# A filter stage unrolled in half tiles, and two thirds of a modulation product moved to VectorE in a late stage

## The reference, cut to what matters

```
mod_lat = jnp.split((jax.nn.silu(c) @ w_mod[l] + b_mod[l])[:, None, :], 6, axis=-1)
mod_ctx = jnp.split(jax.nn.silu(c_ctx) @ w_mod[l] + b_mod[l], 6, axis=-1)
u_ctx = modulate(h_ctx, mod_ctx[0], mod_ctx[1])
mix_lat, _ = token_mixer(modulate(h_lat, mod_lat[0], mod_lat[1]), ctx_states, lp, rows)
h_lat = layer_norm(DN_ALPHA * h_lat + mod_lat[2] * mix_lat, ln_g[l, 0], ln_b[l, 0])
ffn_lat = moe_ffn(modulate(h_lat, mod_lat[3], mod_lat[4]), lp)
h_lat = layer_norm(DN_ALPHA * h_lat + mod_lat[5] * ffn_lat, ln_g[l, 1], ln_b[l, 1])

def hyena_filters(n, lp):
    hid = jnp.sin(lp["hy_freq"][0] * (feat @ lp["hy_w1"] + lp["hy_b1"]))     # feat (n, 33), hid (n, 64)
    hid = jnp.sin(lp["hy_freq"][1] * (hid @ lp["hy_w2"] + lp["hy_b2"]))
    filt = (hid @ lp["hy_w3"]) * jnp.exp(-t01 * deltas)                      # (n, 2048)
    filt = filt.reshape(n, HY_ORDER, 2, HY_D)
    fwd, bwd = filt[:, :, 0], filt[:, :, 1]
    k2 = jnp.concatenate([fwd, jnp.zeros((1, HY_ORDER, HY_D), F32), jnp.flip(bwd[1:], axis=0)], axis=0)
    return k2 / jnp.sum(jnp.abs(k2), axis=0, keepdims=True)
```

## Time and profile before

| what | value |
|---|---|
| median of the runs | 3189.16 us (3187.28 to 3192.15) |
| span of the profiled execution, first to last instruction | 3182.9 us |
| TensorE busy in the span | 2769.4 us, 87% |
| VectorE busy | 1631.1 us, 51% |
| ScalarE busy | 996.2 us, 31% |
| GpSimd busy | 279.9 us, 9% |
| mean granted TensorE clock | 0.928 |
| first matmul of `stage_filter_spectrum` (L578) starts at | 188.09 us |
| stretch of the `md` merge | about 2010 to 2152 us |

### The profile page before, as it was taken

The page is one execution under the profiler, slowest core; times in us unless marked ns, Lnnn a source line. Parts: engine busy times, 40 slices in busy tenths (PEclk is TensorE's granted clock), DMA queues, the critical chain, the costliest instruction groups (busy, mean ns, idle before and its releaser), DMA issues. The chain is left out here.

```text
span 3182.9 us, 33378 instructions
## 1 busy us (share of the span) xinstructions
PE 2769.4 (87%) x12400; PEld 2050.8 (64%) x12400; DVE 1631.1 (51%) x1517; ACT 996.2 (31%) x1104; POOL 279.9 (9%) x236
## 2 busy tenths in 40 slices
PE   7889898989999599999894999998918999999973
PEld 4443773335888577878773778784417888888861
DVE  4634336272332256343178262424627888888866
ACT  2302230001332133320000010001007888888860
POOL 1200000000000221000141300000010000000001
PEclk9889999999999788999996999998958999999996
DMA  6432454221232421211110111113149999999945
GB/s 213 132 126 112 166 205 135 89 86 60 67 108 84 135 78 52 71 53 51 40 51 14 47 34 47 43 30 121 50 189 366 371 375 374 371 371 371 373 183 224
DMA packets 92001, 482.89 MB, mean 152 GB/s; under 512 B 10836, under 2 KB 20324, under 8 KB 76745
## 3 DMA queue, kind: packets, MB, share of 16 engines
q1 hardware_dynamic: 71688, 382.41, 33.5%
q0 software_dynamic: 20224, 99.25, 8.3%
HBM read 424.01 MB, written 82.78 MB: 159 GB/s over the span
## 5 line engine op out<-in xcount | busy, mean ns | idle before, releaser
L337 PE MATMUL ps<-uT_upper_rest,ring_rest 128*128 128x512 f32 x1360 | 541.3, 398 | 0.0
L337 PEld LDWEIGHTS ps<-uT_upper_rest,ring_rest 128*128 128x128 f32 x1360 | 259.0, 190 | 66.1
L337 PE MATMUL ps<-uT_upper_rest,cs_upper 128*128 128x512 f32 x320 | 130.2, 407 | 55.0 <-DVE cs_val L1971 46.8
L2443 PE MATMUL ps<-ring_rest,uT_rest 128*128 128x256 f32 (+1 forms) x416 | 135.2, 325 | 26.2 <-DVE uT_upper_rest L2520 26.2
L2445 PE MATMUL ps<-ex_u_raw_rest,uT_rest 128*128 128x256 f32 x560 | 156.6, 280 | 0.0
L2443 PE MATMUL ps<-ex_upper,uT_rest 128*128 128x256 f32 (+1 forms) x424 | 136.3, 322 | 21.0 <-DVE uT_upper_rest L2520 21.0
L337 PE MATMUL ps<-uT_upper_rest,xbc_upper 128*128 128x512 f32 x336 | 136.0, 405 | 6.1 <-DVE ring_rest L727 6.1
L1744 PE MATMUL ps<-sb_merged,ring 128*128 x256 | 114.5, 610 | 26.0 <-DVE sb_merged L1819 26.0
L2444 PE MATMUL ps<-ex_upper,uT_rest 128*128 128x256 f32 (+1 forms) x424 | 134.3, 317 | 0.0
L337 PE MATMUL ps<-uT_rest,xbc_upper 128*128 128x512 f32 x336 | 134.2, 399 | 0.0
L2444 PE MATMUL ps<-ring_rest,uT_rest 128*128 128x256 f32 (+1 forms) x416 | 133.3, 320 | 0.0
(11 more groups left out here) (437 smaller groups left out, 6305.6 us busy)
## 6 DMA issues: line engine op xcount, KB each, us to landing
sb_spare<-in_ex_g SPq DMA_DIRECT2D x35, 2048.0 KB
ex_u_raw<-in_ex_u SPq DMA_DIRECT2D x35, 2048.0 KB
sb_merged<-in_ex_d SPq DMA_DIRECT2D x35, 2048.0 KB, 10.3
ring<-in_w_mod SPq DMA_DIRECT2D x48, 512.0 KB, 4.5
sb_uT<-moe SPq DMA_DIRECT2D x35, 512.0 KB, 12.0
moe<-sb_uT POOLq DMA_DIRECT2D x35, 512.0 KB, 8.0
ring<-in_w_gate SPq DMA_DIRECT2D x32, 512.0 KB, 3.6
ring<-in_dft SPq DMA_DIRECT2D x24, 512.0 KB, 3.6
```

The source lines that it names most:

```text
L337: last = self.nc.tensor.matmul(out, weight, x[:, k, lo:hi], start=(k == 0 and n == 0), stop=(k == kt - 1 and n == 2))
L2443: nc.tensor.matmul(out, left_up, w_up, start=first, stop=False)
```

## The change: what it does, and the diff

The filter stage loses its hardware loop. It is written out in 16 turns, each half a tile: 128 tokens for one of the two filter orders, so 1024 of the 2048 columns. The hidden layers hold tokens 0 to 511 on partitions 0 to 63 and tokens 512 to 1023 on partitions 64 to 127, so the chain of VectorE has 512 columns on 128 partitions; `w2` and `w3` are stored twice, once for each half. The copy to `hid_t` is gone: TensorE takes its weights from `hid` directly. `window`, `filt` and `mags` have two buffers, PSUM three pairs of banks. The scaling of the first tap is done in tile 0 alone. The exponentials for tiles 0 and 1 go ahead of the turns, each later one two tiles ahead. The loads have semaphores of their own: the first layer waits for four small ones.

Only 16 of the 48 modulation items (vectors 0 and 1) are computed there. Their weights are the ring's first segment. Vectors 2 to 5 are accumulated in the `md` merge: GpSimd's queue loads 32 pieces of 128x1024 (512 KB), VectorE multiplies each with a column of `ccs` and adds it to a tile `late` (four rows of 1024 on each partition, with the bias on partition 0). `late` takes the place of `y_aT`, which now lives on through the tail, where the output stage sums its partitions with a matrix of ones and writes the four rows back over it.

```
 @@ stage_filter_time, sync
-                for dst, src in loads:
-                    sp.dma_start(dst, src).then_inc(loaded, 16)
+                for dst, src in ((featT[:, :], a["featT"]), (w1[:, :], a["hy_w1"]), (k.cols[:, :], a["cols"]),
+                                 (w2[:, :], a["hy_w2"])):
+                    sp.dma_start(dst, src).then_inc(feat_in, 16)
+                sp.dma_start(w3[:, :], a["hy_w3"]).then_inc(w3_in, 16)
+                sp.dma_start(k.consts[:, :], a["consts"]).then_inc(consts_in, 16)
+                sp.dma_start(deltas[:, :], a["neg_deltas"][0].partition_broadcast(P)).then_inc(deltas_in, 16)
                 ring.stream(sp)
 @@ tensor
+                def modulation(m):
+                    slot = m % RING
+                    ring.arrived(pe, base, m // RING, slot)
+                    if m >= 4 and m % 2 == 0:
+                        pe.wait_ge(mod_read, m // 2 - 1)
+                    for kt in range(KT):
+                        mm = nc.tensor.matmul(ps[0:2, 6 + m // 2 % 2, (m % 2) * P:(m % 2 + 1) * P], k.ccs[:, kt, :],
...
+                def filters(n):
+                    t, o = halves[n]
+                    h, at = t // 4, t % 4 * P
+                    part = slice(h * HY_HID, (h + 1) * HY_HID)
+                    if n >= 3:
+                        pe.wait_ge(filt_read, n - 2)
+                    for d in range(2):
+                        q = 2 * o + d
+                        mm = nc.tensor.matmul(ps[:, 2 * (n % 3) + d, :], hid[part, 1, at:at + P],
+                                              w3[part, q * HY_D:(q + 1) * HY_D], start=True, stop=True)
+                    mm.then_inc(filt_mm, 1)
...
+                pe.wait_ge(hid_ready, 2)
+                pe.wait_ge(w3_in, 16)
+                for n in range(len(halves)):
+                    filters(n)
+                    if n + 4 < EARLY:
+                        modulation(n + 4)
 @@ scalar
+                decay(0)
+                decay(1)
+                modulated(0)
+                modulated(1)
+                for n in range(len(halves)):
+                    act.wait_ge(filt_ready, n + 1)
+                    if n >= 2:
+                        act.wait_ge(summed, n)
+                    nc.scalar.activation(mags[:, n % 2, :, :], filt[:, n % 2, :, :], ACT.Abs).then_inc(mags_ready, 1)
+                    if n % 2 and n // 2 + 2 < TT:
+                        decay(n // 2 + 2)
+                    if n % 2 and n // 2 + 2 < EARLY // 2:
+                        modulated(n // 2 + 2)
 @@ vector
+                for n, (t, o) in enumerate(halves):
+                    mine = filt[:, n % 2, :, :]
+                    v.wait_ge(filt_mm, n + 1)
+                    v.wait_ge(window_ready, t + 1)
+                    if n >= 2:
+                        v.wait_ge(mags_ready, n - 1)
+                        v.wait_ge(folded, 2 * (n - 1))
+                    nc.vector.tensor_tensor(mine, ps[:, 2 * (n % 3):2 * (n % 3) + 2, :],
+                                            window[:, t % 2, 2 * o * HY_D:2 * (o + 1) * HY_D].rearrange(
+                                                "p (d c) -> p d c", d=2), ALU.mult).then_inc(filt_read, 1)
...
                     for dst, op in ((even, ALU.add), (odd, ALU.subtract)):
+                        nc.vector.tensor_tensor(dst[:, t, o, :], mine[:, 0, :], mine[:, 1, :], op).then_inc(folded, 1)
 @@ stage_merge
+                if late is not None:
+                    pool.wait_ge(late_zero, 1)
+                    lo, hi = ROW_AT["b_late"]
+                    pool.dma_start(late[0:1, :, :].rearrange("p q n -> p (q n)"), a["rows"][:, lo:hi]).then_inc(late_b, 16)
+                    for i in range(KT):
+                        for q in range(LATE):
+                            if i:
+                                pool.wait_ge(late_done, LATE * (i - 1) + q + 1)
+                            pool.dma_start(piece[:, q, :], a["w_late"][i * LATE + q]).then_inc(late_in[q], 16)
...
+                def late_modulation(i):
+                    for q in range(LATE):
+                        v.wait_ge(late_in[q], 16 * (i + 1))
...
+                        nc.vector.scalar_tensor_tensor(out=late[:, q, :], in0=piece[:, q, :], scalar=k.ccs[:, i, 0:1],
+                                                       in1=late[:, q, :], op0=ALU.mult, op1=ALU.add).then_inc(late_done, 1)
                 split_items(0)
+                if late is not None:
+                    nc.vector.memset(late[:, :, :], 0.0).then_inc(late_zero, 1)
...
                         split_items(i + 1)
+                    if late is not None:
+                        late_modulation(i)
                     merge(i)
 @@ stage_output
-                for part in range(4):
-                    for kt in range(KT):
-                        m = (2 + part) * KT + kt
-                        mm = nc.tensor.matmul(ps[:, 2 * part + kt // 4, (kt % 4) * P:(kt % 4 + 1) * P],
-                                              k.mod[:, m, 0:1].broadcast_to([P, P]), k.const("ident"),
+                for part in range(LATE):
+                    for h, (lo, hi) in enumerate(HALVES):
+                        mm = nc.tensor.matmul(ps[:, 2 * part + h, :], k.ones[:, :], rows[:, part, lo:hi],
                                               start=True, stop=True)
```

More of the change, by code:

```diff
@@ L63 @@
 KTILES = TT // 2
+EARLY = 2 * KT
+LATE = 4
 BIG = 1e30
@@ L375, in stage_filter_time @@
-        arg, whole = sb("arg", [HY_HID, T]), sb("whole", [HY_HID, T])
-        hid, hid_t = sb("hid", [HY_HID, 2, T]), sb("hid_t", [HY_HID, P])
-        window = k.spare[:, 0:2, :].rearrange("p k t -> p (k t)")
-        filt, mags, mag_sum = (k.spare[:, 2 * i:2 * i + 2, :].rearrange("p o (d c) -> p o d c", d=2) for i in range(1, 4))
-        loaded, cc_in, silu_c = sem("loaded"), sem("cc_in"), sem("silu_c")
+        cc = sb("cc", [P, KT, 2])
+        arg, whole = sb("arg", [P, T // 2]), sb("whole", [P, T // 2])
```

208 lines of the change are left out of this document (99 added, 109 removed).

## The result

| what | before | after |
|---|---|---|
| median of the runs | 3188.22 us (3183.95 to 3192.15, 4 runs) | 3099.06 us (3094.86 to 3104.45, 4 runs) |
| ratio | | 0.9724, 95% interval 0.9709 to 0.9740 |
| span of the profiled execution | 3182.9 us | 3093.3 us |
| VectorE busy in the span | 1631.1 us | 1637.1 us |
| TensorE busy in the span | 2769.4 us | 2681.0 us |

The changed kernel is 89.6 us shorter by the spans. The filter stage gave 80.2 of them; 79.1 were forecast.

The account below looks back on a forecast made before the run. The prediction saw a chain in the filter stage, no engine full, and TensorE bounding the md merge. Span 3182.9 - 79.1 (filter stage) = 3103.8, plus 6.3 to the median, gave 3110 us; range 3096 to 3132.

Parts of the forecast that it names:

- The chain: Filter stage before the change: no engine is full, engines wait for each other, 17.4 us from one turn to the next.
- item 1's landing: Start of the filter stage: modulation item 1's weights land at 15.3 us, uncertain by -1.5 to +6 us.
- The gap of 4 us before item 4: Filter stage, turns 0 and 1: TensorE idles 4 us because item 4 stands behind a read-out that follows ScalarE's windows.
- The low clock behind it: After TensorE's first-turn gap: item 4 takes 2.1 us and filters(1) 3.6 us, ending at 35.6.
- the lock between fold and add: Turns 2 to 15: VectorE's fold and GpSimd's add run in series, only the fold charged: 3.85 us a turn.
- The tail: Filter stage's end: partition sum 5.93 us, reciprocal 6.56, then 1.4 to the next stage's first matmul at 109.0.
- The merge and the output stage: Work moved into the md merge (between 0 and 8 us) and the output stage's new records: both costed at nothing.
- the wait of 6.3 us: md merge: after four multiply-adds of 4.9 us, 6.3 us remain of VectorE's 11.23 us wait for TensorE.
- the rival of late pieces: md merge: pieces arriving one after another at 8.0 us each make turns 39 us instead of 16.8: 3264 us; chance 3%.
- The low clock: Rival: TensorE stays at 1.2 GHz, turns 2 to 11 take 5.6 us instead of 3.85, 17 us more: 3127; chance 15%.
- The case without lock: Rival: no lock between VectorE and GpSimd, turns of 3.6 and 2.9 us, or a warm tail: 3102 us; chance 17%.
- The stages between are untouched: Stages between the filter stage, the md merge and the output stage: no change in time counted.

Follow-up runs that it names:

- unroll_only: Kernel before with only the filter stage unrolled, all 48 modulation items kept there and the old output stage: 3160.20 us, ratio 0.9920.
- early_readout: Changed kernel with ScalarE reading out the first two pairs of modulation items before its windows: 3096.82 us, ratio 0.9732.
- pe_sums: Changed kernel with the magnitudes of the last four half tiles summed by TensorE instead of GpSimd: 3089.74 us, repeated 3091.15 us, ratio 0.9716 both times.
- no_late: Changed kernel without the 32 late modulation pieces (output not the reference's, 32 expert blocks): 3043.14 us, ratio 0.9563.
- late_only: Kernel before with only the modulation moved: hardware loop kept, no items in it, 32 pieces in the md merge: 3185.34 us, ratio 1.0009.
- few_items: Changed kernel with one of eight matmuls in modulation items 4 to 15 (output not the reference's, 34 expert blocks instead of 35): 3080.89 us, ratio 0.9685.
- pad_layout: Changed kernel with 320 unused bytes a partition, so the tensors behind lie at their old SBUF addresses: 3105.86 us, ratio 0.9757.
- the kernel with both edits: Changed kernel with ScalarE's early read-outs and TensorE's sums of the last four half tiles' magnitudes: 3098.09 us, ratio 0.9734; repeated 3095.85 us, ratio 0.9726.

## Why the prediction was right, point by point

*The bound and the start.* The chain was read rightly: `unroll_only` shows that taking it apart turns the stage into one bound by TensorE. The first layer was forecast at 5.0 us (4.90) with 3.67 for its matmuls (1.97), the second sine's end at 24.4 (25.96). VectorE's chain took 4.4 us as reckoned. Item 0 was there early (13.46 against 15.3), but the first two items kept TensorE until 19.87 instead of 17.1: their records take 6.41 us, the next two items' 3.65. It is a slower TensorE and not item 1's landing: the median record of these two items takes 417 ns, that of item 4 at 0.50 takes 418, and that of items 2 and 3 at 1.00 takes 272. (The first stretch above prints 1.00 for this time all the same.) The gap of 4 us before item 4 came as said (3.57). The low clock behind it was priced too low: item 4 took 3.57 us and not 2.1, since the 8.46 of the earlier trace rows for four items was not at the low clock throughout; the clock was back within filters(1), which took 2.53 instead of 3.6. It ended at 37.6 (35.6 forecast) and the second add at 42.93 (41.3).

*The turns.* 3.85 us each were forecast (the terms as written, 1.38 + 2.34 + 0.1, make 3.82), 3.75 measured, by another reason than the one given. The prediction let the lock between fold and add set the pace, "a little above TensorE". In the steady turns TensorE sets it, with 1.98 + 1.91 less an overlap, and the add fits between the folds. The two are almost equal: folds of 1.29 and an add of 2.45 in series make 3.74. That the number held is luck. Two runs show the lock's own price: 4.06 a turn in `early_readout`, more than the parts in series, and 2.59 where it is absent in the tail of `pe_sums` (2.9 was reckoned). The Trainium skill (SBUF — State Buffer, section "Who interferes with whom") has that a VectorE instruction with two SBUF inputs and a GpSimd instruction that reads SBUF shut each other out; the folds of 0.69 us against 2.83 agree. The same page of the Trainium skill leaves out instructions with at most one SBUF input only where they are outside VectorE's two-port modes. The product, with one input from PSUM and one from SBUF, keeps its 1.22 us while an add runs. Two instructions with a single SBUF input lose time, so the exception counts here: the scaling of the first tap in `early_readout`, beside an add, took 1.38 us instead of 0.49, and the copy of the kernel before took 4.52 or 4.53 us in seven turns, behind an add, and in the first turn, without one, 0.22:

```profile
41.24 0.22 DVE L509 COPY ft_hid_t<-ft_hid 64x128 f32 x1 [1.34 <-ACT ft_hid L463]
```

So charging only the fold was right for what is left in the turns, but the prediction didn't see that the copy which the change removes was itself held up by GpSimd's add: that wait was a link of the old chain.

*The tail.* The last add ended at 94.61 us against 95.2, the sum took 5.16 instead of 5.93, and the next stage began at 107.87 against 109.0. The turns that TensorE no longer paced are where the lock did cost: `pe_sums` won back 4 to 5 us there.

*The merge and the output stage* were costed at nothing, and are: the wait of 6.3 us was met with 6.36, and `no_late` shows the same 156.1 us without the work. A late piece landed 4.3 us after its issue (median), so the rival of late pieces had less to stand on than the 8.0 of the earlier trace rows.

*The rivals.* The low clock didn't stay: 0.93 over the turns. But it was nearer than its 15% said. `late_only` and `few_items` both stay at 0.50 for the rest of the filter loop once most items are gone. `few_items` differs from the changed kernel in nothing else, so there it was the whole item behind every half product that brought the clock back. And the rival's price was too low: it took 5.6 us a turn (3.6 + 2.1 make 5.7), but at 1.2 GHz a half product takes 3.78 and an item 3.57, some 7.2 with their overlap, so ten turns would have cost about 33 us and not 17, by this estimate outside the range. The Trainium skill (TensorE: Matmul & The Clock Gate, section "HAM oscillation — how this bites in real kernels") has repeated waits bring the clock down. The fall agrees: it comes in the gap of 3.57 us. But in `few_items` TensorE counts as busy for all of 16 us between 60 and 76 and the clock is low all the same, so waits are not the whole of it. The case without lock forecast a total of 3102, nearer to the result than the 3110 on record, but not by its mechanism: the lock is there.

*The size.* Of the 11 us between 3110 and 3099, the stage itself explains 1.1, and 0.5 the step from the span to the median (6.3 assumed, 5.8 measured; a single run is only 1.6 above its own span, so most of this term is that the profiled execution was a quick one, both times). The term that failed is "The stages between are untouched": in work they are, but what lies behind the filter stage became 9.4 us shorter. `pad_layout` gives back 8 or 9 us of time with the old addresses alone, by medians (6 to 8 by the ratios, whose intervals overlap), and 8.0 of the 9.4 us lie in the stretch from the first merge to the output stage, which goes with the addresses in 14 traces. Some 1 to 2 us of these can be the output stage's new start: from the `md` merge's first matmul to the first output matmul it is 157.6 us padded, and 158.7 to 159.4 where the old start stands at the same addresses.

## What to carry to other kernels

Take a chain apart before taking work off an engine that only fills its waits: alone, the moved modulation gave nothing and the unrolling 24 us, and together they gave 86 to 89. Work that lies in a wait can be worth keeping, since it may be what holds TensorE's clock up; removing it slowed the same matmuls from 1.98 to 3.78 us. Where VectorE and GpSimd alternate on SBUF, look at when in the turn the add falls, and give the last sums to an engine that is idle then.

## What was not expected of the hardware

A shift of SBUF addresses by 320 bytes changed the pace of float32 matmuls of 512 columns from 397 to 393 or 394 ns in merges that the change doesn't touch, and a stretch of some 900 us by 5 to 9 us (4 traces against 10); the medians of the whole kernel differ by 8 or 9 us, 0.3%. What in the addresses decides was not tried.

The lock has a steady pattern that is slower than its parts in series: once a fold had met an add, turns went in pairs of 8.13 us, where folds and add one after the other would take 3.74 each. Both traces of the kernel with both edits, the same up to the last four half tiles, had none of it.

TensorE was granted 1.2 GHz in turns in which it counted as busy throughout (`few_items` between 60 and 76 us, with one matmul of an item between the half products); with the item's eight matmuls there, in the changed kernel, the same products ran at 2.4 GHz. What in the items decides was not tried.

A copy of 64x128 numbers with a single SBUF input took 0.22 us alone and 4.52 behind an add of GpSimd: not only VectorE's two-input instructions wait.
